# Two transformer blocks on one core: x loaded in halves on two queues, high parts multiplied first, and split turns at each norm

## The chip, the cores and the metric

The kernel runs on one core of one Trainium2 chip, in one launch. The metric is the device time of that launch in microseconds (us), as the median of several runs. TensorE (PE) multiplies, VectorE (DVE) and ScalarE (ACT) do elementwise work, GpSimd (POOL) does some elementwise work and issues transfers, SyncE (SP) issues transfers. All numbers are float32.

## The reference

256 rows of 1024 features pass through two blocks. The first block has two layers, the second one has one; every stage adds to the residual h.

```python
hn = rmsnorm(h, mix_norm[0])                 # y = x * rsqrt(mean(x*x) + eps) * g
h = h + moba_nsa_mixer(hn, ...)              # 8 causal heads + 8 heads of three gated branches
h = h + sqrelu_mlp(rmsnorm(h, ...), w1, w2)  # relu(h @ w1)**2 @ w2, 4096 hidden
h = h + fox_mixer(rmsnorm(h, ...), ...)      # 16 heads with a forget bias
h = h + sqrelu_mlp(rmsnorm(h, ...), w1, w2)
h = rmsnorm(h, final_norm)
# second block: shifts, scales and gates come from silu(c) @ w_ada + b_ada
h = h + 0.5 * gt1 * swiglu(modulate(rmsnorm(h, g1), sh1, sc1), ...)       # 2816 hidden
h = h + gt2 * hybrid_mixer(modulate(rmsnorm(h, gm), sh2, sc2), ...)       # pooling + dilated attention
h = h + 0.5 * gt3 * swiglu(modulate(rmsnorm(h, g2), sh3, sc3), ...)
out = rmsnorm(h, g_final)
```

In the three-branch (NSA) heads, each branch's softmax is multiplied by its own gate, sigmoid of a projection; one branch attends to 15 compressed blocks. With 256 rows, the block selections select everything that is causal.

## The kernel before, in words

The rows are two tiles of 128 (t = 0, 1). Weights arrive as 174 units of 128 x 2048 float32 (1 MB) in a ring of four buffers; unit u is loaded as soon as unit u - 4 has been used (`unit_used`). A float32 product is made of three passes in fp32r: every operand is split into a high part (rounded) and a low part (the rest), and high x low, low x high and high x high are summed (`three`, L1531 to L1534; L1563 and L1564 in the wide form). ScalarE rounds the weights (`round_half`, half a unit, L683; `advance`, a whole unit, L694), VectorE subtracts to get the rest (`rest_half`, L1050; L1061). `hi_ready` and `lo_ready` count the halves done.

Each norm needs, for each row tile: sums of squares on ScalarE (L705), a root and some polishing on VectorE (`inverse_root`), the scaling of the rows (`scale`: L1100 on VectorE in the first norm, L761 on ScalarE in the others, in pieces of 256, 256 and 512 columns), the turn of the rows by eight transposes in four chunks of 256 features (`turn_rows`, L1630), and out of the turned banks a high part on ScalarE (L746, or L748 and L753 where a shift is added) and a low part on VectorE (L1167, or L1154 and L1163). `act_high` counts high parts, `act_split` counts low parts, a chunk at a time. In the first norm ("mix0") the chunks of both row tiles are interleaved.

The products right behind a norm are `first_rows` (before the MLP and SwiGLU stages, through `begin_hidden`) and the value units (`value_part`, through `begin_values`, before the mixers; the first mixer, `v_even`, has its own order in the program of TensorE, L1772 to L1788). All of them wait for a chunk's low part before its first product, and the turn of row tile 1 stands in one piece among the products of row tile 0.

The opening: SyncE issues x's tile 0, the two halves of the first weight unit and x's tile 1 (L520 to L524), then further units. ScalarE issues the small tables, GpSimd the tables of the relative bias. Until the data land, TensorE does 22 warm-up products (L1774).

A mixer runs in ticks (a half or a quarter of a unit each). A plan, `plan`, writes out for each tick which heads' scores are made (`s`), which are turned (`t`), which are multiplied with the values (`pv`) and which output tiles are closed (`closed`); a closed tile is split by ScalarE (L838) and VectorE (L1253) one tick later. In a tick VectorE first does the logits of the tick's heads (L1226), then copies, weight halves, reciprocals, `extras`, and closed tiles. For the 16 gated heads VectorE multiplies the sum of the exponentials by 1 + exp(-z) and takes the reciprocal (L1246, L1247); GpSimd multiplies the probabilities by it (L565). The compressed branch has extras: its scores are taken over and shifted at tick ("km0", 2) (L1426 to L1433), exponentiated and weighed at ("km0", 3) (L959, L1434 to L1445), and turned by TensorE at the ticks of `CT_AT` (L1859).

## Time and profile before

| | us |
|---|---|
| median of three runs | 1103.0 (1101.99 to 1103.15) |
| the profiled execution's own time | 1100.71 |
| its span, first to last instruction | 1098.9 |
| TensorE busy | 1075.3 |
| VectorE busy | 779.2 |
| ScalarE busy | 662.0 |

The profile is of one execution. Times in the rows count from the first instruction. A row of the timeline has its start, its length, the engine, the line, the operation, what it writes and reads, its shape, and in square brackets the idle time of that engine just before it with what ended it. Rows of the same line that follow one another are merged (x8), and a matmul's length is modelled and overlaps the next.

### The profile page before, as it was taken

The page shows a single profiled execution, that of the slowest core. Times are in us where ns is not written, and L with a number is a line of the kernel's source. Part 1 is how long each engine was busy: PE and PEld are TensorE (multiplying, and loading weights), DVE is VectorE, ACT ScalarE, POOL GpSimd, SP SyncE. Part 2 cuts the span into 40 slices and gives each one's busy share as a digit, 9 for nine tenths or more (in the row PEclk, how much of TensorE's full clock was granted, in tenths as well). Part 3 has the DMA queues.
Part 4 walks back from the last instruction along what each step waited for, and adds up shares of the span by engine and source line. Part 5 has one row for each costly group of instructions (what it writes and reads, how often), then busy time and mean ns, then how long its engine had stood idle before and what let it go on. Part 6 is the DMA issues. An engine that isn't in the chain of part 4 may idle for free.

```text
span 1098.9 us, 15922 instructions
## 1 busy us (share of the span) xinstructions
PE 1075.3 (98%) x6102; PEld 915.4 (83%) x6102; DVE 779.2 (71%) x1272; ACT 662.0 (60%) x1071; POOL 112.8 (10%) x209
## 2 busy tenths in 40 slices
PE   8999999999999999999999999999999999999997
PEld 7988788888888997888888788888878977888885
DVE  6667667877777776676766778887875766565566
ACT  6667677565576776766565764354475766444443
POOL 1032201010100531020000000101000100000000
PEclk9999999999999999999999999999999999999999
DMA  8842348878764632687778457768545445555551
GB/s 337 298 160 78 116 154 319 301 283 316 289 217 174 227 123 108 210 322 267 273 254 340 153 204 284 295 253 318 198 153 178 149 144 182 191 191 181 185 185 65
DMA packets 40620, 238.31 MB, mean 217 GB/s; under 512 B 4661, under 2 KB 5845, under 8 KB 17632
## 3 DMA queue, kind: packets, MB, share of 16 engines
q1 hardware_dynamic: 26784, 188.81, 48.1%
q0 software_dynamic: 13040, 47.85, 11.6%
q8 instruction: 49, 0.80, 0.3%
q10 hardware_dynamic: 720, 0.62, 0.2%
q14 instruction: 27, 0.22, 0.1%
HBM read 236.15 MB, written 1.11 MB: 216 GB/s over the span
## 4 chain that ended last, share of the span: by engine, by line
PE 80%; DVE 9%; ACT 6%; issue 3%; DMA 1%; DVEq 0%; SPq 0%; ACTq 0%
PE bank L1563 21%; PE bank L1532 15%; PE bank L1534 14%; PE bank L1533 14%; PE bank L1564 10%; DVE w_lo L1061 2%; PE bank L1726 1%; PE bank L1708 1%; DMA raw<-in_stream 1%; DVE ada_raw L1296 1%; DVE w_lo L1050 1%; ACT w_hi L683 1%; ACT w_hi L694 1%; PE bank L1700 1%; ACT tok L705 1%
## 5 line engine op out<-in xcount | busy, mean ns | idle before, releaser
L1563 PE MATMUL bank<-a_two,w_hi 128*128 128x512 f32 x1088 | 386.9, 399 | 0.8 <-DVE w_lo L1061 0.8
L1061 DVE TENSOR_TENSOR w_lo<-raw,w_hi 128x2048 fp32r<-128x2048 f32 x122 | 278.5, 2303 | 105.3 <-ACT w_hi L694 105.3
L1564 PE MATMUL bank<-a_two,w_lo 128*128 128x256 f32 x1088 | 305.3, 281 | 0.0
L694 ACT ACTIVATE w_hi<-raw 128x2048 fp32r<-128x2048 f32 x122 | 232.2, 1910 | 63.0 <-DMA raw<-in_stream 62.9
L1563 PEld LDWEIGHTS bank<-a_two,w_hi 128*128 128x128 f32 x1088 | 204.4, 188 | 51.1 <-issue 1.3
L1564 PEld LDWEIGHTS bank<-a_two,w_lo 128*128 128x128 f32 x1088 | 205.5, 189 | 1.7
L1532 PE MATMUL bank<-w_lo,hid_hi 128*128 128x512 f32 x432 | 169.5, 392 | 0.1
L1533 PE MATMUL bank<-w_hi,hid_lo 128*128 128x512 f32 x432 | 168.6, 390 | 0.0
L1534 PE MATMUL bank<-w_hi,hid_hi 128*128 128x512 f32 x432 | 168.4, 390 | 0.0
L866 ACT ACTIVATE cross<-bank 128x256 f32<-128x256 f32 x136 | 51.5, 381 | 187.0 <-PE bank L1564 186.6
L1050 DVE TENSOR_TENSOR w_lo<-raw,w_hi 128x1024 fp32r<-128x1024 f32 x104 | 125.4, 1224 | 25.5 <-ACT w_hi L683 25.0
L683 ACT ACTIVATE w_hi<-raw 128x1024 fp32r<-128x1024 f32 x104 | 106.5, 1050 | 21.2 <-DMA raw<-in_stream 20.9
L1532 PEld LDWEIGHTS bank<-w_lo,hid_hi 128*128 128x128 f32 x432 | 81.1, 188 | 18.9 <-DVE hid_lo L1268 1.0
L1534 PEld LDWEIGHTS bank<-w_hi,hid_hi 128*128 128x128 f32 x432 | 81.1, 188 | 17.8
L1533 PEld LDWEIGHTS bank<-w_hi,hid_lo 128*128 128x128 f32 x432 | 81.1, 188 | 15.2
L1532 PE MATMUL bank<-a_two,w_hi 128*128 128x256 f32 x320 | 93.5, 292 | 0.0
L1534 PE MATMUL bank<-a_two,w_hi 128*128 128x256 f32 x320 | 90.4, 283 | 0.0
L1533 PE MATMUL bank<-a_two,w_lo 128*128 128x256 f32 x320 | 90.4, 282 | 0.0
L1296 DVE CUSTOM_DVE_ANT_0 ada_raw<-ada_raw,silu_row 128x1024 f32<-128x1024 f32 x72 | 84.8, 1219 | 5.2 <-DMA ada_raw<-in_ada 3.5
L1261 DVE TENSOR_TENSOR hid_act<-bank,cross 128x256 f32<-128x256 f32 x96 | 39.1, 420 | 56.5 <-ACT cross L866 56.5
L580 POOL DMA_DIRECT2D ada_raw<-in_ada x72 | 38.1, 530 | 325.9 <-DVE modc L1296 325.9
L1532 PE MATMUL bank<-w_lo,a_two 128*128 128x512 f32 (+1 forms) x160 | 62.1, 388 | 6.1 <-DVE a_two L1167 3.0
(215 smaller groups left out, 1490.3 us busy)
## 6 DMA issues: line engine op xcount, KB each, us to landing
raw<-in_stream SPq DMA_DIRECT2D x173, 1024.0 KB, 4.9
ada_raw<-in_ada POOLq DMA_DIRECT2D x72, 512.0 KB, 5.1
cmpw<-in_stream SPq DMA_DIRECT2D x4, 1024.0 KB, 7.0
rel_band<-rel_scratch POOLq DMA_DIRECT2D x2, 1024.0 KB, 10.6
cum_row<-cum_scratch POOLq DMA_DIRECT2D x4, 512.0 KB, 5.3
gate_row<-gate_scratch POOLq DMA_DIRECT2D x3, 512.0 KB, 5.6
h<-in_x SPq DMA_DIRECT2D x2, 512.0 KB, 5.9
raw<-in_stream SPq DMA_DIRECT2D x2, 512.0 KB, 6.6
```

Of the source, the lines that this page charges most:

```text
L683: nc.scalar.activation(w_hi[:, u % RING, part_], raw[:, u % RING, part_], ACT.Copy).then_inc(hi_ready, 1)
L694: nc.scalar.activation(w_hi[:, u % RING, :], raw[:, u % RING, :], ACT.Copy).then_inc(hi_ready, 2)
L866: nc.scalar.activation(cross[:, slot, nt, :], ps[bank][:, T:2 * T], ACT.Copy).then_inc(done, 1)
L1050: nc.vector.tensor_tensor(w_lo[:, u % RING, part_], raw[:, u % RING, part_], w_hi[:, u % RING, part_].bitcast(F32), ALU.subtract).then_inc ...
L1061: nc.vector.tensor_tensor(w_lo[:, u % RING, :], raw[:, u % RING, :], w_hi[:, u % RING, :].bitcast(F32), ALU.subtract).then_inc(lo_ready, 2)
L1261: nc.vector.tensor_tensor(to[:, nt * T:(nt + 1) * T], ps[bank][:, 0:T], cross[:, slot, nt, :], ALU.add).then_inc(done, 1)
L1296: nc.vector.tensor_tensor_reduce(part, part, silu_row[:, :], 1.0, 0.0, ALU.mult, ALU.add, modc[:, p:p + 1]).then_inc(ada_done, 1)
L1532: nc.tensor.matmul(dst, l_hi, r_lo, start=start, stop=False)
L1533: nc.tensor.matmul(dst, l_lo, r_hi, start=False, stop=False)
L1534: return nc.tensor.matmul(dst, l_hi, r_hi, start=False, stop=stop)
L1563: nc.tensor.matmul(ps[bank][:, 0:2 * T], wh[:, k, cols_], a_two[:, :, k, :], start=k == 0, stop=False)
L1564: ins = nc.tensor.matmul(ps[bank][:, T:2 * T], wl[:, k, cols_], a_hi[:, k, :], start=False, stop=k == KT - 1)
```

## The change

- x is loaded in four pieces (row tile by column half): the first halves on SyncE's queue, the second ones on ScalarE's, where the bias pick table and the second half of the first weight unit go too. VectorE takes the squares of tile 0's second half. Both tiles are scaled before the first chunk is turned.
- In the opening, `first_value` is now `opening`: it does the terms of one k and one row tile in a given order; "h" is high x high, "r" is high x low weights, "l" is low x high weights. Only "l" waits for the chunk's low part. `first_rows` does the two high terms before it waits for the low part.
- Tile 1's turn is in two calls, chunks 0 and 1 and chunks 2 and 3, with part of the last chunk of tile 0 ahead of and between them.
- With a shift, VectorE does a shift and a low part in turn.
- `close_tiles` moves the second of two tiles closed in one tick to the next tick, except in the last two ticks.
- The gate is kept as 1 / (1 + exp(-z)) and is a second factor in GpSimd's operation.
- The compressed branch's steps are one or two ticks later.
- 19 warm-up products in place of 22.

```diff
-WARM = 22
+WARM = 19
@@ close_tiles
+    for tick, later, last in reversed(list(zip(ticks, ticks[1:], ticks[2:]))):
+        if len(tick.closed) == 2:
+            later.closed = [tick.closed.pop()] + later.closed
...
-CT_AT = [("km1", 0, 1), ("km1", 0, 2), ("qm1", 0, 0), ("qm1", 0, 1)]
+CT_AT = [("km1", 0, 2), ("km1", 0, 3), ("qm1", 0, 0), ("qm1", 0, 1)]
@@ SyncE
-            sp.dma_start(h[:, 0, :], x[0:P, :]).then_inc(x_landed[0], 16)
-            for part in range(2):
-                part_ = slice(HALF * part, HALF * part + HALF)
-                sp.dma_start(raw[:, 0, part_], stream[0][:, part_]).then_inc(first_landed[part], 16)
-            sp.dma_start(h[:, 1, :], x[P:T, :]).then_inc(x_landed[1], 16)
+            sp.dma_start(h[:, 0, 0:512], x[0:P, 0:512]).then_inc(x_landed[0][0], 16)
+            sp.dma_start(h[:, 1, 0:512], x[P:T, 0:512]).then_inc(x_landed[1][0], 16)
+            sp.dma_start(raw[:, 0, 0:HALF], stream[0][:, 0:HALF]).then_inc(first_landed[0], 16)
@@ GpSimd
-                        ins = pool.tensor_scalar(p_, p_, wgt[:, 2 * i + t:2 * i + t + 1], 1.0, ALU.mult, ALU.mult)
+                        gate = 1.0 if heads[i][5] is None else gates[:, t, heads[i][5]:heads[i][5] + 1]
+                        ins = pool.tensor_scalar(p_, p_, wgt[:, 2 * i + t:2 * i + t + 1], gate, ALU.mult, ALU.mult)
@@ ScalarE, opening
+            act.dma_start(h[:, 0, 512:D], x[0:P, 512:D]).then_inc(x_landed[0][1], 16)
             act.dma_start(par[:, 0:COLS["pool_scale"]], cols[:, 0:COLS["pool_scale"]]).then_inc(norms_landed, 16)
             act.wait_ge(dve_step, 1)
+            nc.scalar.activation(stat[:, 10, :], stat[:, 9, :], ACT.Sqrt)
+            act.dma_start(h[:, 1, 512:D], x[P:T, 512:D]).then_inc(x_landed[1][1], 16)
+            act.dma_start(rpick[:, :], rel_pick).then_inc(pick_landed, 16)
+            act.dma_start(raw[:, 0, HALF:UNIT], stream[0][:, HALF:UNIT]).then_inc(first_landed[1], 16)
-            squares("mix0", 0)
+            act.wait_ge(x_landed[0][0], 16)
+            nc.scalar.activation(tok[:, 0, 0:512], h[:, 0, 0:512], ACT.Square, scale=1.0 / 32, accum_out=stat[:, 0, 0:1]).then_inc(sumsq, 2)
+            root("mix0", 0)
+            square_half("mix0", 1, 0)
+            square_half("mix0", 1, 1)
+            root("mix0", 1)
...
-                if tick.at("km0", 0, 3):
+                if tick.at("km1", 0, 0):
                     act.wait_ge(cshifted, 1)
@@ VectorE, turned
-                if shift is not None and chunks[0] == 0:
-                    for c in (1, 3):
+                for c in chunks:
+                    if shift is not None and c < 2:
+                        odd = 2 * c + 1
...
@@ VectorE, mixer: 16 gated heads
-                            chain(nc.vector.tensor_tensor(w, inv_gates[:, :, gate], d, ALU.mult))
-                            nc.vector.reciprocal(w, w).then_inc(weight_ready, 1)
+                        nc.vector.reciprocal(wgt[:, 2 * i:2 * i + 2], den[:, 2 * i:2 * i + 2]).then_inc(weight_ready, 1)
@@ VectorE, opening
+            dve.wait_ge(x_landed[0][1], 16)
+            chain(nc.vector.tensor_tensor_reduce(tok[:, 0, 512:D], h[:, 0, 512:D], h[:, 0, 512:D], 1.0 / D, 0.0, ALU.mult, ALU.add,
+                                                 stat[:, 1, 0:1]))
             inverse_root("mix0", 0)
             scale("mix0", 0)
+            inverse_root("mix0", 1)
+            scale("mix0", 1)
             rest_half()
...
-                if tick.at("km0", 0, 2):
+                if tick.at("km0", 0, 3):
                     dve.wait_ge(cscores, 1)
-                if tick.at("km0", 0, 3):
+                if tick.at("km1", 0, 1):
                     dve.wait_ge(cprobs, 1)
@@ TensorE, first_rows
+                pe.wait_ge(act_high, TURN[name] + 4 * t + 2 * j + half + 1)
+                for k in [2 * half + n for n in ks]:
+                    nc.tensor.matmul(dst, a_hi[:, 4 * j + k, ts], wh[:, k, :], start=j == 0 and k == 0, stop=False)
+                    nc.tensor.matmul(dst, a_hi[:, 4 * j + k, ts], wl[:, k, :], start=False, stop=False)
                 pe.wait_ge(act_split, TURN[name] + 4 * t + 2 * j + half + 1)
...
@@ TensorE, begin_hidden
-                turn_rows(name, 1)
-                first_rows(name, u, 1, 0, 1)
+                first_rows(name, u, 1, 0, 1, (0,))
+                turn_rows(name, 1, (0, 1))
+                first_rows(name, u, 1, 0, 1, (1,))
+                turn_rows(name, 1, (2, 3))
@@ TensorE, begin_values: in the same way with opening(..., ns=(0,)) and opening(..., ns=(1,))
...
@@ TensorE, opening of v_even
-            first_value(j=0, part=0)
-            first_value(j=0, part=1)
-            pe.wait_ge(pick_landed, 32)
+            pe.wait_ge(pick_landed, 16)
+            pe.wait_ge(relt_landed, 16)
             pe.wait_ge(pool_step, 1)
             nc.tensor.matmul(ps[6][0:16, 0:REL], relt[:, :], rpick[:, :], start=True, stop=True).then_inc(rel_rows, 1)
+            first_value = partial(opening, "mix0", "v_even", width=V1W)
+            first_value(0, 0, 0, "h")
             turn_rows("mix0", 1)
+            first_value(0, 0, 0, "rl")
+            first_value(0, 0, 1, "hlr")
             pe.wait_ge(rel_rows_sb, 1)
+            first_value(0, 1, 0, "hr")
+            first_value(0, 1, 1, "hr")
+            first_value(0, 1, 0, "l")
+            first_value(0, 1, 1, "l").then_inc(unit_used, 1)
+            for k in range(2):
+                for t in range(TT):
+                    ins = first_value(1, t, k)
+            ins.then_inc(unit_used, 1)
```

## Rows read from the trace of the kernel before

**Rows 1.** The page, busy time of each engine, its share, instructions.

```profile
PE 1075.3 (98%) x6102; PEld 915.4 (83%) x6102; DVE 779.2 (71%) x1272; ACT 662.0 (60%) x1071; POOL 112.8 (10%) x209
```

**Rows 2.** Windows: length; busy PE, PEld, DVE, ACT, POOL; granted clock, DMA share, GB/s.

```profile
4.50:6.00 1.50, 1.50 (x15) 1.50 (x15) 0.15 (x1) 1.29 (x4) 1.36 (x1) 1.00 1.00 235
...
14.00:16.60 2.60, 0.77 (x8) 0.56 (x6) 0.77 (x3) 2.60 (x7) 0.49 (x1) 1.00 0.97 404
```

**Rows 3.** Timeline of all engines, 0 to 30 us.

```profile
4.71 0.63 ACT L705 ACTIVATE tok<-h 128x512 f32<-128x512 f32 x1 [2.04 <-DMA h<-in_x]
...
7.18 0.88 DVE L1100 TENSOR_SCALAR tok<-h,stat 128x512 f32<-128x512 f32 x2
7.19 1.06 ACT L683 ACTIVATE w_hi<-raw 128x1024 fp32r<-128x1024 f32 x1 [0.75 <-DMA raw<-in_stream]
...
8.28 1.23 DVE L1050 TENSOR_TENSOR w_lo<-raw,w_hi 128x1024 fp32r<-128x1024 f32 x1 [0.21 <-ACT w_hi L683]
8.54 0.62 ACT L746 ACTIVATE a_two<-bank,par 128x128 fp32r<-128x128 f32 x2 [0.30 <-PE bank L1630]
...
9.42 0.60 DVE L1167 SCALAR_TENSOR_TENSOR a_two<-bank,par,a_two 128x128 fp32r<-128x128 f32 x2
...
10.08 0.50 PE L1532 MATMUL bank<-w_lo,a_two 128*128 128x512 f32 x1 [1.20 <-DVE a_two L1167]
...
13.66 1.09 PE L1630 MATMUL bank<-par,tok 128*128 128x128 f32 x8
...
16.59 0.47 PE L1532 MATMUL bank<-w_lo,a_two 128*128 128x512 f32 x1 [1.83 <-DVE a_two L1167]
...
24.00 2.28 DVE L1061 TENSOR_TENSOR w_lo<-raw,w_hi 128x2048 fp32r<-128x2048 f32 x1
```

**Rows 4.** The tile h in 0 to 15 us: its two transfers.

```profile
DMA to landing us min/median/max: 3.9/5.9/7.8
```

**Rows 5.** Windows as in rows 2, and ScalarE's timeline, unit 6.

```profile
24.00:26.00 2.00, 2.00 (x13) 1.75 (x12) 2.00 (x2) 1.15 (x2) 0.00 (x0) 1.00 0.73 229
...
35.03 1.06 ACT L683 ACTIVATE w_hi<-raw 128x1024 fp32r<-128x1024 f32 x1 [4.69 <-DMA raw<-in_stream]
```

**Rows 6.** TensorE's timeline at the turn of tile 1, norm mlp0.

```profile
150.05 0.83 PE L1630 MATMUL bank<-par,tok 128*128 128x128 f32 x4
...
151.05 0.66 PE L1630 MATMUL bank<-par,tok 128*128 128x128 f32 x4 [0.17 <-ACT tok L761]
151.47 0.47 PE L1532 MATMUL bank<-w_lo,a_two 128*128 128x512 f32 x1
```

**Rows 7.** Timelines of TensorE and ScalarE in the norm gmix.

```profile
816.51 0.50 PE L1532 MATMUL bank<-w_lo,a_two 128*128 128x512 f32 x1 [0.75 <-DVE a_two L1163]
...
821.32 0.84 PE L1630 MATMUL bank<-par,tok 128*128 128x128 f32 x4 [0.42 <-ACT tok L761]
...
823.00 0.72 ACT L753 ACTIVATE a_two<-shifted 128x256 fp32r<-128x256 f32 x2
...
824.22 0.42 PE L1532 MATMUL bank<-w_lo,a_two 128*128 128x512 f32 x1
```

**Rows 8.** Timelines of TensorE and VectorE, even mixer, ticks km0 and km1.

```profile
84.38 0.84 DVE L1429 TENSOR_TENSOR pc<-bank,pc 128x240 f32<-128x240 f32 x2
...
86.80 0.36 PE L1699 MATMUL bank<-k_two,q_two 128*128 128x256 f32 x1 [1.42 <-DVE low L1226]
...
88.00 0.40 DVE L1437 TENSOR_REDUCE den<-pc 128x16 f32<-128x240 f32 x1
...
92.24 0.60 PE L1859 MATMUL bank<-par,pc 128*15 128x128 f32 x4
```

**Rows 9.** Timelines of VectorE and TensorE, fox mixer.

```profile
414.32 0.76 DVE L1253 TENSOR_TENSOR q_two<-bank,q_two 128x256 fp32r<-128x256 f32 x2
...
415.78 0.36 PE L1699 MATMUL bank<-k_two,q_two 128*128 128x256 f32 x1 [1.07 <-DVE low L1226]
```

**Rows 10.** GpSimd's timeline, even mixer.

```profile
88.16 0.83 POOL L565 TENSOR_SCALAR prob<-prob,wgt 128x256 f32<-128x256 f32 x2 [3.69 <-DVE wgt L1247]
```

More of the change, by code:

```diff
@@ L1593, in turn_hidden, with row_part @@
                 ins.then_inc(hid_turned, 1)
-            def row_part(u, banks, l_hi, l_lo, width, start, stop, part, parts, by_rows=False, sums=False, opening=False):
+            def row_part(u, banks, l_hi, l_lo, width, start, stop, part, parts, by_rows=False, sums=False):
                 wh = w_hi[:, u % RING, 0:2 * width].rearrange("p (k c) -> p k c", k=2)
@@ L1599, in row_part @@
                 four = [(t, n) for t in range(TT) for n in range(2)]
-                if opening:
-                    order = [(k, t, n) for t in range(TT) for k in range(2) for n in range(2)]
-                elif by_rows:
+                if by_rows:
                     order = [(k, t, n) for t, n in four for k in range(2)]
@@ L1937, in _ @@
             mlp("mlp0", "mix1")
-            begin_values("mix1", lambda j, part: value_part("mix1", "v_fox", j, part, 4))
+            begin_values("mix1", "v_fox")
             def fox_extras(tick):
@@ L1960, in _ @@
             glu("glu0", "gmix")
[L1961 removed]
+            begin_values("gmix", "uv_dil")
             def dil_extras(tick):
```

106 lines of the change are left out of this document (56 added, 50 removed).

## The prediction

> **What bounds the kernel now.** I read the page's busy shares first: TensorE is busy for 1075.3 of the 1098.9 us span and VectorE for 779.2 [rows 1]. A matmul's modelled end overlaps its successor, so the share alone hides waits. I therefore read the list of who waited for whom and then TensorE's timeline at the places it names. Steady 512-column products start 0.228 us apart, 256-column ones 0.118 us, and against that pitch the trace has few gaps: the opening, the half turn that repeats in each norm, and some waits inside the two attention mixers. Everywhere else a change on another engine is worth nothing. The change touches exactly these places.
>
> The opening is a latency chain. The first x tile lands at about 4.7, its squares, root and scaling run until 8.06, eight transposes, a rounding and a split follow, and the first product starts at 10.08 [rows 3]. x's second tile, issued behind both weight halves, lands 7.8 us after its issue at 2.11 [rows 4]. Its turn starts at 13.66 and its product at 16.59; TensorE does 0.77 us of work in 14.0 to 16.6 [rows 2, 3]. From 16.59 it streams without a gap to the end of v_even at 31.8, 15.2 us for three and a half units, so 4.34 a unit (0.36 for one term of one k and one row tile).
>
> **Opening, part by part.** x goes in four pieces of 256 KB on two queues, ahead of the weights. The first two together are the 512 KB that now land at 4.7, so I keep 4.7 for them. The other two come 0.35 and 0.6 MB later. The windows show 235 GB/s in 4.5 to 6.0 and 404 in 14.0 to 16.6 [rows 2], so I put tile 1 whole at 6.7 to 7.4, against 9.9 now. The price: 0.5 MB of x, the small tables and half of the other queue now stand ahead of the first weight half, which today lands at 7.15 [rows 3]; at 400 GB/s that is 8.0 to 9.4.
>
> VectorE takes one half of tile 0's squares. Nearest is its own 128x512 multiply with sum, 0.69 in the fused norm, beside ScalarE's 0.63 plus 0.19: both are done by 5.5, where two ScalarE halves end at 6.05 now. Root, reciprocal and two polishing steps take 1.0; tile 0 is scaled from 6.8, tile 1's root follows, and tile 1 is scaled by 9.9 to 10.2 (two halves take 0.88). Then ScalarE rounds the first half (1.06) [rows 3] from 8.2 to 9.4, turns chunk 0 (0.62), rounds the second half, copies the bias rows (0.59) and turns tile 1's chunk. The first product needs only the rounded half and the high part, so it starts at 10.0 to 11.1, no earlier than now. Tile 1's turn comes right behind it at 10.3 to 11.5, against 13.66.
>
> VectorE becomes the late one. In order it owes: the rest of half 1 (1.22), chunk 0's split (0.60), the rest of half 2, two more chunk splits, then the rests of unit 1 with a split between [rows 3]. That gives unit 0 done at 15.5 (early landing) or 16.1 (late), against 16.59 plus 2.15 = 18.7. Units 1 and 2 follow at 4.34 each; unit 3 waits for its 2.28 us rest, which starts at 24.0 now [rows 3] and would start at 21.9 or 22.9. End of v_even: 28.6 or 29.6, against 31.8. The opening saves 3.2 or 2.2; I take 2.6.
>
> What is late next: the weights of unit 6, for which ScalarE waits 4.69 us until 35.03 [rows 5]. Their issue waits for unit 2, so it moves with TensorE, and the queues are not full in 24 to 26 (229 GB/s) [rows 5]; by the same bytes they land at about 32. ScalarE's and VectorE's full stretch from there to the first scores at 52.7 shifts with it. I take off 0.1 for what is not passed on: 2.5. Bounds 0.5 (everything lands 2 us later than I say) and 4.
>
> The three warm-up products fewer end at about 6.9; nothing waits for them. The rest of the weight halves moved one slot is a reordering of equal work.
>
> **The half turn, six times.** In every norm after the first, TensorE turns tile 1 in one go: four transposes in 0.40, then it stands until ScalarE has scaled columns 512 to 1023, then four more. At 150.05 the second four start at 151.05: 0.60 idle, and 151.47 is the next product [rows 6]. Now one k of the last chunk (0.69) goes ahead of the turn and one k between its halves. In mlp0, mix1 and mlp1 TensorE reached the turn with everything ready, so the whole 0.60 is covered: from 150.05, product to 150.74, four transposes to 151.14, product to 151.83, transposes to 152.25; today that point is 151.47 + 1.38 = 152.85. Tile 1's high part would be ready by 151.65 and its split by 152.2, where the first products need it at 152.25 and, with high parts first, only at 153.2. 3 x 0.60 = 1.8.
>
> In gf1, gmix and gf2 there is a shift too. The first product of tile 0 waits for the low part: in gmix it starts at 816.51 [rows 7], 1.14 behind the product before it, of which 0.91 is not pitch. With high parts first that wait goes, but it buys nothing by itself: the turn of tile 1 waits for ScalarE's scaling at 821.32 [rows 7], and that chain starts from sums and squares which TensorE no longer drives. The idle time moves from ahead of tile 0 to ahead of the turn. What is gained is behind it: tile 1's first product waits now for work order (824.22) and then for ScalarE's rounding of chunk 0, 823.00 + 0.37 plus a hop, 823.5 [rows 7]: 0.72. The same reading gives 0.80 in gf1 (632.79 against 631.98) and 0.74 in gf2 (911.64 against 910.90). VectorE's shifts now stand between the splits, which delays its later adds by 0.08, counted. Sum 2.3; with the others 4.1. Bounds: 3.0 if the later steps hand back 0.2 each, 5.0 if the first waits count too.
>
> **Mixers.** Fox: two closed tiles cost VectorE 0.76 ahead of the logits for which TensorE waits 1.07 [rows 9]. Closing one there and one a tick later takes off 0.38; the deferred one falls in front of logits that are not awaited. 0.4. In the dilated mixer no wait follows its double close: 0.
>
> Even: the compressed scores' four operations (84.38 to 86.10) stand ahead of the logits that cost TensorE 1.42 at 86.80 [rows 8]. A tick later they wait for nothing, and that 1.42 goes, as does 0.60 at 91.88 behind it. But the weighing of the compressed heads, 1.93 from 88.00 [rows 8], moves two ticks while its reader moves one. By my count VectorE reaches it at 93.1 and ends at 95.05; TensorE gets to the transposes at 93.4 and stands 1.7. Net 2.0 - 1.7 - 0.2 of logits = 0.1. Bounds -0.8 and +1.6.
>
> The gate goes from VectorE (one chained operation of about 0.2 for each of 16 heads) to a second per-row scalar on GpSimd. Its two operations take 0.83 [rows 10] and their reader comes 5 us later, so neither saving nor a doubling reaches the path: 0, between -0.5 and +0.3.
>
> **Sum.** 2.5 + 4.1 + 0.4 + 0.1 = 7.1. On the profiled execution (span 1098.9, its time 1100.7) that is a span of 1091.8. The median of the three runs is 1103.0, 2.3 above the profiled time; I take the difference as it is: 1095.9.
>
> **A rule about two queues.** The Trainium skill, DMA: Bandwidth & Descriptors, Issuing engines are not separate DMA queues, says that transfers started by different engines share the same 16 DMA engines and interleave, so that a second starter only saves issue time. By that rule the second queue lands nothing sooner in total, and x's halves are paid for by the weights: the late end of my opening, 2.2. The trace has only tiny transfers on the second queue and neither confirms nor contradicts it.
>
> **Rivals.**
> The opening gives nothing. First product no earlier, weights later, VectorE full. For it: the order of VectorE's list, and 2 KB rows where there were 4 KB. Against: tile 1 is now missing for 3.7 us and that is removed in every version. Saving 0.3 + 4.6 = 4.9: 1098.1.
>
> The even mixer takes it back. The stall at the transposes grows when unit weights arrive late: up to 0.8 net loss, and with the opening at 2.0: 5.7 saved, 1097.3.
>
> The clock falls in the opening, the case on the slower side. TensorE would stand with short work between 6.9 and 13. If it were granted half speed there and kept it while v_even streams, the 15.2 us of work from 16.59 to 31.8 would take 30.4: 1103.0 - 7.1 + 15.2 = 1111. The balance is nought where 7.1 us of full-speed work, about half of that stretch, run at 1.2 GHz. Against it: 1.00 is granted from the start and through 14.0 to 16.6 [rows 2], with a stand of 1.8. The new stands are each no longer. The Trainium skill, TensorE: Matmul & The Clock Gate, What's actually happening, says that half speed is the idle state and that activity lifts it; the granted clock in these rows never shows that state.
>
> The change doesn't do what it says: the transfers on ScalarE's queue go out only behind its table load (1.28) and land as late as now. Then tile 1 lands at 9.9 and blocks ScalarE's first rounding; the opening saves 1: 1097.4.
>
> **Chances.** Forecast 0.60, opening gives nothing 0.12, even mixer 0.10, late second queue 0.10, clock 0.03; 0.05 for what I don't see. A measurement tells 0.2% (2.2 us) from nothing. The likeliest case alone runs from 1094 to 1098; with the unknown bounds (savings of 3.4 to 9.8) the range is 1093.2 to 1099.6. Faster 0.89, same 0.07, slower 0.04.
>
> **What would show it.** Tile 1's transposes at 10.3 to 11.5 and v_even's end before 30; no idle between the halves of tile 1's turn in six norms; in the three shifted norms an idle stretch of about 1 us ahead of that turn; the 1.42 at the even mixer gone and one of 1 to 2 us ahead of the compressed transposes. It is wrong if v_even ends past 31, if the granted clock drops, or if the first score of the even mixer keeps its place though v_even ends early.

## The result and the profile after

The changed kernel takes 1107.2 us (median of 14 runs, 1103.67 to 1109.66), the kernel before 1102.67 in the same session: ratio 1.0035, 95% interval 1.0025 to 1.0046. It is slower by 0.35%; 1095.9 was forecast. All fourteen executions have a mean granted clock of 0.991 to 0.997; the two at 0.997 took 1103.7 and 1104.2, the others 1105.0 to 1109.7. The profiled execution took 1107.36 us.

The page of the changed kernel; the busy line answers to [rows 1]. TensorE is busy 2.5 us more, for the same products, and the span is 6.5 longer.

```profile
span 1105.4 us, 15921 instructions
...
PE 1077.8 (98%) x6096; PEld 918.8 (83%) x6096; DVE 778.3 (70%) x1259; ACT 664.3 (60%) x1069; POOL 113.9 (10%) x208
```

The list of who waited for whom on TensorE (total, times, longest). The first, second, fourth and fifth rows were not there before: TensorE waits for the weights' rest `w_lo` in `first_rows` (L1592) and `opening` (L1700), for the relative-position pick, and for the compressed heads' probabilities `pc`.

```profile
PE bank L1592 <- DVE w_lo L1062: 5.0, 4, 2.1
PE bank L1818 <- DMA rpick<-in_rel_pick: 3.0, 1, 3.0
PE bank L1748 <- ACT probT L822: 2.1, 2, 1.9
PE bank L1700 <- DVE w_lo L1062: 1.8, 2, 1.5
PE bank L1903 <- DVE pc L1455: 1.4, 1, 1.4
```

**The opening.** The tile h: four transfers now, from 3.7 to 9.1 us from issue to landing, where [rows 4] had 3.9 to 7.8.

```profile
DMA to landing us min/median/max: 3.7/4.1/9.1
```

TensorE's timeline, answering to [rows 3] (turn of tile 0, pick, first product, turn of tile 1, end of v_even).

```profile
7.39 1.06 PE L1644 MATMUL bank<-par,tok 128*128 128x128 f32 x8 [0.44 <-DVE tok L1112]
11.44 1.88 PE L1818 MATMUL bank<-rpick,relt 33*16 33x511 f32 x2 [2.99 <-DMA rpick<-in_rel_pick]
13.53 1.00 PE L1700 MATMUL bank<-w_hi,a_two 128*128 128x512 f32 x2 [0.21 <-ACT a_two L748]
14.33 1.91 PE L1644 MATMUL bank<-par,tok 128*128 128x128 f32 x8
...
33.71 0.28 PE L1543 MATMUL bank<-a_two,w_hi 128*128 128x256 f32 x1
```

ScalarE's timeline. It stands 4.19 us for x's last quarter, then 1.78 for the second weight half.

```profile
10.81 0.63 ACT L707 ACTIVATE tok<-h 128x512 f32<-128x512 f32 x1 [4.19 <-DMA h<-in_x]
...
15.17 1.06 ACT L685 ACTIVATE w_hi<-raw 128x1024 fp32r<-128x1024 f32 x1 [1.78 <-DMA raw<-in_stream]
```

Windows, columns as in [rows 2]. The granted clock (the third number from the end) goes to 0.50, which is 1.2 GHz, late in a stand of TensorE from 8.5 to 11.4. In [rows 2] it was 1.00 at 14.0 to 16.6. v_even ends at 33.71 instead of 31.81.

```profile
9.00:10.00 1.00, 0.00 (x0) 0.00 (x0) 0.00 (x0) 0.00 (x0) 0.00 (x0) 1.00 1.02 422
10.00:12.00 2.00, 0.56 (x1) 0.12 (x2) 0.21 (x1) 1.09 (x4) 0.00 (x0) 0.71 1.02 419
12.00:14.00 2.00, 1.79 (x3) 0.50 (x2) 1.86 (x6) 1.39 (x3) 0.00 (x0) 0.50 1.04 428
14.00:16.60 2.60, 2.60 (x12) 2.40 (x12) 1.56 (x4) 1.43 (x2) 0.00 (x0) 0.50 0.99 410
```

**The norms.** TensorE at tile 1's turn in mlp0, answering to [rows 6]. The idle between the halves is gone, but 152.76, the product now ahead of the turn, starts 0.59 behind its pitch (0.82 behind the product before it, where 0.23 is usual), waiting for `w_lo`.

```profile
151.71 0.61 PE L1596 MATMUL bank<-w_hi,a_two 128*128 128x512 f32 x2
152.76 0.50 PE L1592 MATMUL bank<-w_hi,a_two 128*128 128x512 f32 x1 [0.43 <-DVE w_lo L1062]
...
153.57 0.60 PE L1644 MATMUL bank<-par,tok 128*128 128x128 f32 x4
```

VectorE makes that `w_lo` only behind tile 1's inverse root, whose last operation starts at 151.41:

```profile
151.48 1.22 DVE L1062 TENSOR_TENSOR w_lo<-raw,w_hi 128x1024 fp32r<-128x1024 f32 x1
```

TensorE in gmix, answering to [rows 7]. The product waits until 825.41, and the turn starts at 825.98. ScalarE starts scaling the tile at 824.25. Before, the turn was at 821.32; this stage starts 3.49 later here, so that is 824.81 in this trace, and the turn is 1.17 late. Counted in the same way it is 1.43 late in gf1 and 1.40 in gf2.

```profile
822.73 1.14 PE L1700 MATMUL bank<-w_hi,a_two 128*128 128x512 f32 x3
825.41 0.50 PE L1700 MATMUL bank<-w_lo,a_two 128*128 128x512 f32 x1 [1.53 <-DVE w_lo L1062]
...
825.98 0.60 PE L1644 MATMUL bank<-par,tok 128*128 128x128 f32 x4
...
827.51 1.06 PE L1644 MATMUL bank<-par,tok 128*128 128x128 f32 x4
```

The clock falls behind that stand too, and in gf2 from 915 to 919, but not in gf1, where the stand is 2.1:

```profile
823.00:825.00 2.00, 0.85 (x3) 0.19 (x1) 1.32 (x4) 1.25 (x4) 0.00 (x0) 1.00 0.19 78
...
827.00:829.00 2.00, 2.00 (x8) 1.61 (x7) 1.16 (x5) 1.75 (x5) 0.13 (x1) 0.50 0.00 0
```

**Mixers.** A wait of 1.40 at the compressed transposes ([rows 8]) came as forecast, and the fox wait ([rows 9]) fell from 1.07 to 0.74. The stretch that holds it (to mlp1, below) is only 0.15 to 0.2 shorter by the fox edit: 115.74 to 115.55 in e4, 115.32 to 115.17 from e3 to e8.

```profile
97.31 0.61 PE L1903 MATMUL bank<-par,pc 128*15 128x128 f32 x4 [1.40 <-DVE pc L1455]
...
417.55 0.36 PE L1739 MATMUL bank<-k_two,q_two 128*128 128x256 f32 x1 [0.74 <-DVE low L1238]
```

**Where the time went.** TensorE's timeline cut at v_even's end, at tile 0's turn in each norm, and at the last product. Lengths in us; three of the columns are experiments told below, and e13 has the mixers' edits too.

| stretch | before | change | norms only (e2) | rest last (e3) | both mended (e13) |
|---|---|---|---|---|---|
| start to v_even's end | 31.81 | 33.71 | 32.30 | 33.45 | 29.25 |
| to mlp0 | 111.88 | 112.10 | 112.65 | 113.99 | 112.09 |
| to mix1 | 180.55 | 180.67 | 180.67 | 180.22 | 180.18 |
| to mlp1 | 115.74 | 115.43 | 115.57 | 115.32 | 115.17 |
| to gf1 | 182.19 | 182.63 | 182.49 | 182.30 | 182.15 |
| to gmix | 190.54 | 191.66 | 191.52 | 190.62 | 190.53 |
| to gf2 | 87.40 | 88.79 | 88.95 | 87.30 | 87.29 |
| to the last product | 191.13 | 192.68 | 193.33 | 190.96 | 191.10 |

The opening costs 1.90, the last three rows, behind the norms with a shift, 4.06.

### The profile page after: what moved, and what is told of

Its sections match the earlier page's. It is cut to its first block, busy times and chain, and to the rows that moved or that the text cites. A ratio compares the mean times of both kernels' runs of the same rounds, so it can differ in the third digit from the quotient of the medians.

```text
span 1105.4 us, 15921 instructions
## 1 busy us (share of the span) xinstructions
PE 1077.8 (98%) x6096; PEld 918.8 (83%) x6096; DVE 778.3 (70%) x1259; ACT 664.3 (60%) x1069; POOL 113.9 (10%) x208
## 3 DMA queue, kind: packets, MB, share of 16 engines
q10 hardware_dynamic: 1196, 1.74, 0.4%
## 4 chain that ended last, share of the span: by engine, by line
PE 79%; DVE 10%; ACT 5%; issue 3%; DMA 2%; ACTq 0%; SPq 0%; DVEq 0%
PE bank L1574 19%; PE bank L1543 13%; PE bank L1545 13%; PE bank L1544 13%; PE bank L1575 10%; PE bank L1700 2%; DVE w_lo L1073 2%; DMA raw<-in_stream 2%; ACT w_hi L696 2%; DVE w_lo L1062 2%; PE bank L1766 1%; PE bank L1748 1%; DVE ada_raw L1303 1%; ACT tok L707 1%; DMA h<-in_x 1%
## 5 line engine op out<-in xcount | busy, mean ns | idle before, releaser
L1574 PEld LDWEIGHTS bank<-a_two,w_hi 128*128 128x128 f32 x1088 | 204.4, 188 | 51.2 <-issue 1.5
L1544 PEld LDWEIGHTS bank<-w_hi,hid_lo 128*128 128x128 f32 x432 | 81.1, 188 | 15.2
L1543 PEld LDWEIGHTS bank<-a_two,w_hi 128*128 128x128 f32 x320 | 61.1, 191 | 2.1 <-issue 1.9
```

What stands on the lines that cost most here:

```text
L1543: nc.tensor.matmul(dst, l_hi, r_lo, start=start, stop=False)
L1544: nc.tensor.matmul(dst, l_lo, r_hi, start=False, stop=False)
L1574: nc.tensor.matmul(ps[bank][:, 0:2 * T], wh[:, k, cols_], a_two[:, :, k, :], start=k == 0, stop=False)
```

## The experiments

All parts below are hunks of the change's own diff put on the kernel before, unless a diff or a sentence says otherwise. The ratios are to the kernel before on the same chip.

**e1: the new opening alone.** Edit: the transfers, the order of both halves and of the terms in mix0, `WARM = 19`.

> The kernel before with the new opening alone (x in four pieces on two queues, high parts first, VectorE's half of the squares, 19 warm-up products); norms, mixers and gate as before. Theory A, from the changed kernel's trace: what is put on ScalarE's queue is starved (x's last quarter lands at 10.8, the relative-position pick at 11.4, the second weight half at 15.2), TensorE stands, its clock falls to half from about 11 to 17, and v_even ends at 33.7 instead of 31.8; of these 1.9 us some 1.3 to 2.1 reach the end: 1104.0 to 1104.8, ratio 1.0012 to 1.0019. Rival B: the opening's loss is hidden by ScalarE's wait of 4.7 us for weights, and the whole loss is the norms': 1102.7 within 0.5. The prediction on record would have 1100.2.

Measured: 1.0001 (0.9991 to 1.0012). x's last quarter is used at 10.26, v_even ends at 34.25, the clock is 0.50 from 12 to 19. The mechanism is there, but its loss against the median of the kernel before is not: theory A's time is at the edge of the interval, rival B's holds. e4 shows why.

**e2: the new norm order alone.** Edit: `begin_hidden`, `begin_values`, `first_rows`, VectorE's shifts between the splits.

> The kernel before with the new norm order alone (one k of the last chunk ahead of tile 1's turn, one between its halves, high parts first, shifts between splits); opening, mixers and gate as before. Theory A: the product that was moved ahead of the turn needs the rest of the weights (w_lo) of its half, which VectorE makes only after the inverse root of tile 1; so TensorE waits 0.6 in mlp0, mix1 and mlp1, where it was to save 0.6, and in gf1, gmix and gf2 the turn comes 1.2 to 1.4 late against the work before it. Together 0 from the first three and 1.0 to 1.4 lost in each of the last three, of which part is given back behind: 2 to 4.4 us lost, 1104.7 to 1107.1, ratio 1.002 to 1.004. Rival B, the prediction on record: 4.1 us saved, 1098.6, ratio 0.9963, and the loss of the change is the opening's alone. Rival C: the norms' gain and loss cancel, 1102.7 within 0.5.

Measured: 1.0027 (1.0016 to 1.0037), 3.0 us slower. Theory A; the forecast saving of 4.1 is excluded. TensorE waits for `w_lo` in all six norms: 0.4, 0.2 and 0.4 idle in the first three, 2.1, 1.5 and 2.05 in the shifted ones.

**e3: the rest term last.** The diff is condensed; `begin_values` is changed in the same way.

```
-                first_rows(name, u, 1, 0, 1, (0,))
-                turn_rows(name, 1, (0, 1))
-                first_rows(name, u, 1, 0, 1, (1,))
-                turn_rows(name, 1, (2, 3))
+                if name in SHIFTS:
+                    piece("hl"); turn_rows(name, 1, (0, 1)); piece("r"); turn_rows(name, 1, (2, 3))
+                else:
+                    turn_rows(name, 1, (0, 1)); piece("hl"); turn_rows(name, 1, (2, 3)); piece("r")
```

> As the norm order alone, but the last chunk's products go by term: where there is a shift the high and low rows times the high weights ahead of tile 1's turn and the rows times the weights' rest (w_lo) between its halves; in mlp0, mix1 and mlp1 tile 1's first half is turned first, then the terms with high weights, its second half, then the rest term. Nothing that needs w_lo stands ahead of the turn. Theory A (w_lo is what failed): the 0.60 of each of the first three and the 0.72 to 0.80 of the others come out as forecast, 3.5 to 4.1 us saved: 1098.6 to 1099.2, ratio 0.9963 to 0.9968. Rival B: TensorE stands for another reason (ScalarE's scaling and rounding set tile 1's products in any order), and the result is 1101.5 to 1103.5. Rival C: high parts first or the shifts between the splits cost something by themselves: slower than before by 0.5 us or more.

Measured: 0.9980 (0.9968 to 0.9992), 2.0 us faster. Only the order of the same products and of their waits differs from e2, so the cause of the norms' loss is shown: it is a product that needs `w_lo` ahead of the turn. The saving is half of the forecast. In the table above the stretches behind the norms give less still: e3's are 0.33, 0.42, -0.11, -0.08, 0.10 and 0.17 shorter than before, 0.8 in all, nearly all of it from the first three norms. In mlp0 the turn goes like this, and the second half's turn follows work:

```profile
153.79 0.83 PE L1639 MATMUL bank<-par,tok 128*128 128x128 f32 x4
154.38 1.17 PE L1588 MATMUL bank<-w_hi,a_two 128*128 128x512 f32 x4
155.39 0.60 PE L1639 MATMUL bank<-par,tok 128*128 128x128 f32 x4
```

In the shifted norms the first product of tile 1 comes 2.24 behind its turn, where it came 2.90 behind in gmix before (824.22 against 821.32), but most of it is handed back soon: 0.7 ten us later in gf1 and gf2, and in gmix all but 0.1 by the next norm. In gf1 it is at the turn of the hidden rows:

```profile
644.54 0.44 PE L1601 MATMUL bank<-par,hid_act 128*128 128x128 f32 x2 [0.54 <-DVE hid_act L1304]
```

**e4: the mixers' edits alone.** Edit: `CT_AT` and the compressed heads' ticks, `close_tiles`, `gates` on GpSimd.

> The kernel before with the mixers' three edits alone: tiles closed singly, the compressed heads' steps one or two ticks later, the gate on GpSimd. The prediction on record: fox 0.4 saved, even 0.1 lost or gained, gate 0: 1102.3, ratio 0.9996. From the changed kernel's trace: the even mixer's two waits of 1.4 and 0.6 are gone and a wait of 1.8 at the compressed transposes has come, fox saves 0.33; if the 2.1 us wait for turned probabilities near 64 there comes from weights that land late behind the late opening, it is absent here and the result is 1102.2 within 0.4. Rival: that wait comes from the moved compressed steps or the gate on GpSimd, is here too, and the result is 1103.5 to 1104.5.

Measured: 0.9987 (0.9974 to 1.0). The wait near 64 (1.9 in the change) is absent, as it is in other profiles with either opening: 1.5 to 2.4 in e2, e3, e7, e11, e12 and e15, absent in e1, e5, e6, e8, e10 and e13. From v_even's end to mlp0 this profile has 111.25 and e8's 111.24, against 111.88 before; but e5, which has the old mixer and v_even's end at 32.15 as e8 has it, takes 111.37. So the even mixer saves 0.1 to 0.6. The profile holds the surprise. The opening here is that of the kernel before, yet:

```profile
16.00:18.00 2.00, 0.64 (x2) 0.58 (x3) 1.40 (x3) 2.00 (x7) 0.19 (x1) 0.67 1.04 419
18.00:20.00 2.00, 2.00 (x8) 1.71 (x7) 2.00 (x5) 2.00 (x8) 0.00 (x0) 0.50 0.99 408
...
35.38 0.28 PE L1532 MATMUL bank<-a_two,w_hi 128*128 128x256 f32 x1
```

The clock falls with the stand of 1.83, here from 15.6 to 17.4. In six profiles with the old opening v_even ends at 31.81, 32.15, 32.30, 33.39, 33.45 and 35.38, and the last three have the fall. The profile on which the prediction rests was a lucky one (1100.7, where medians of 1102.3 to 1103.4 were measured).

What such a fall is worth can be read from the mean granted clock of every execution, which is on record for 118 executions of the kernel before on four chips. In 61 of them it is 0.998 or more, with a median time of 1102.0; in 57 it is lower, with a median of 1104.1. The falls, with whatever goes with them, cost 2.1 us in about half of the executions. Against the undisturbed ones on its chip (1101.9) e1, in which no execution reaches 0.998, is 1.6 slower, as its theory A had it.

The three parts alone (e1, e2, e4) multiply to 1.0015, and the whole change is at 1.0035. The 2.2 us between them are within the intervals, and no run explains them.

**e5: the kernel before, its two stands filled.**

```
             turn_rows("mix0", 0)
+            fill(3, 0)
...
             turn_rows("mix0", 1)
+            fill(5, 3)
```

> The kernel before with eight more warm-up products in its opening, three behind tile 0's turn and five behind tile 1's, in the two stands of TensorE (1.2 and 1.8 us in the trace of before). Theory A: the opening of before loses its clock behind the second stand in many executions (two of three profiles of it show 0.5 from about 17 to 20 or 22, v_even ends at 33.5 and 35.4 there, at 31.8 and 32.3 where the clock stays at 1.00), and short work in the stands keeps it: v_even ends near 32 and the median falls by 1 to 2 us, 1101.4 to 1102.4, ratio 0.998 to 0.999. Rival B: the clock falls there whatever TensorE does, 1103.4 within 0.7.

Measured: 0.9987 (0.9975 to 1.0). Clock 1.00 up to the tail, v_even ends at 32.15, runs from 1100.09 to 1102.58 instead of 1100.1 to 1109.3. All twelve executions have a mean clock of 0.998 or more, and their median, 1101.8, is that of the kernel before's undisturbed executions on this chip. Theory A: the ratio is at the interval's edge, and what the fill removes is the executions with a fall.

**e6: the new opening, its transfers elsewhere.**

```
 act: h[:, 0, 512:D]
+act: h[:, 1, 512:D]        (ahead of par and the table load; it stood behind them)
-act: rpick                 +pool: rpick
-act: raw second half       +sp: raw second half, behind the first
```

> The new opening alone, with its transfers put elsewhere: both halves of x for ScalarE's queue ahead of par and the table load, the pick on GpSimd's queue as before the change, the second weight half on SyncE's queue behind the first. Theory A: what stood in the new opening was three transfers starved on ScalarE's queue behind 4 MB of SyncE's; issued early or on the full queue they land in time: x whole by 6.7 to 7.5, second half rounded by 10.5, tile 1's turn at 9.5 to 11, v_even ends at 28.5 to 31, and 1.5 to 2.5 us are saved against the kernel before: 1100.9 to 1101.9. Rival B: the clock falls in the opening all the same and takes the gain back, v_even ends past 31.5: 1102.5 to 1103.5. Rival C: the transfers on ScalarE's queue are as late as they were, x's last quarter past 9.

Measured: 0.9981 (0.9971 to 0.9992), 1100.3 us. ScalarE's and TensorE's timelines, a window of 10 to 12, and what waits at the first scores:

```profile
6.30 0.61 ACT L705 ACTIVATE tok<-h 128x512 f32<-128x512 f32 x1
...
8.52 1.06 ACT L683 ACTIVATE w_hi<-raw 128x1024 fp32r<-128x1024 f32 x1 [0.71 <-DMA raw<-in_stream]
8.82 1.09 PE L1641 MATMUL bank<-par,tok 128*128 128x128 f32 x8 [0.85 <-DMA par<-in_cols]
...
10.80 0.63 PE L1695 MATMUL bank<-w_hi,a_two 128*128 128x512 f32 x2
...
29.07 0.28 PE L1543 MATMUL bank<-a_two,w_hi 128*128 128x256 f32 x1
...
33.77 1.06 ACT L683 ACTIVATE w_hi<-raw 128x1024 fp32r<-128x1024 f32 x1 [4.30 <-DMA raw<-in_stream]
...
51.46 0.36 PE L1732 MATMUL bank<-k_two,q_two 128*128 128x256 f32 x1 [1.47 <-DVE q_two L1215]
```

```profile
10.00:12.00 2.00, 2.00 (x11) 1.16 (x10) 2.00 (x4) 1.70 (x4) 0.00 (x0) 1.00 1.03 434
```

x's last quarter, issued at 1.18, is used at 6.30; in the change it was issued at 1.72, just behind SyncE's first weights (1.65), and landed at 10.8. v_even ends at 29.07, between the forecast's 28.6 and 29.6. But unit 6's weights came only 1.26 sooner (33.77 against 35.03 in [rows 5]), and TensorE stands 1.47 ahead of the first scores: of the 2.74 gained, 1.25 is left at mlp0.

Three transfers moved at once here; e11 and e13 below differ in the order of par and x's last quarter alone. Why it was late can be read from the two queues' packets in the change, here from 8 to 10.8 us (packets, MB, share of the engines' time; q1 is SyncE's, q10 ScalarE's):

```profile
q1 hardware_dynamic: 113, 0.80, 69.3%
q10 hardware_dynamic: 119, 0.33, 29.9%
```

The queues had equal numbers of packets served, but ScalarE's were smaller (2.8 KB on average against 7.1), so it got 29% of the bytes. From 5.5 to 8 it was 129 packets with 0.59 MB against 120 with 0.23 MB. No run changes the size of the packets, so this is read from the trace and not tested.

**e7: the changed norm order, TensorE kept busy.** Eight products are repeated ahead of the one that waits, so the sums are not those of the reference. In gmix it is `opening(..., "h")` four times.

```
+                    for _n in range(8):
+                        nc.tensor.matmul(ps[BEGIN_BANKS[0]][:, :], a_hi[:, 4, 0:P], wh[:, 2, :], start=False, stop=False)
```

> The norm order as changed (as in the run of the norms alone), with eight 128x512 products repeated ahead of the product that waits for w_lo in gf1, gmix and gf2; this changes the sums, and is only for the time. Theory A: the stand of 1.5 to 2.1 us at w_lo lets the clock fall to half behind it (825 to 829 and 913 to 918 in the norms alone), which costs more than the wait itself; with TensorE busy through the stand the clock stays at 1.00 in both and 2 to 3.5 us of the 3.0 that the norms lost come back: 1103 to 1104.3. Rival B: the clock has nothing to do with it, the loss is the wait alone: 1106.3 within 0.7.

Measured: 1.0027 (1.0016 to 1.0038), as e2. The clock did hold: first this kernel in gmix, then e2.

```profile
825.00:827.00 2.00, 2.00 (x12) 1.66 (x11) 0.68 (x2) 1.33 (x4) 0.00 (x0) 1.00 0.00 0
```

```profile
825.00:827.00 2.00, 2.00 (x8) 1.65 (x7) 0.86 (x3) 1.39 (x4) 0.00 (x0) 0.51 0.00 0
```

Its stretches from gmix to the end are 2.1 shorter than e2's, but the ratio is not smaller. The stretches after each norm still sum to 3.1 us over the kernel before. Half of e7's executions, five, have a mean clock of 0.998 or more; their median is 1104.4, 2.6 over the kernel before's undisturbed ones on this chip (1101.8). So with the clock held the wait alone costs 2.6 of the norms' 3.0. The other five have 1106.0: in the profile the clock falls in the opening, which e7 leaves as it was. Theory A's return of 2 to 3.5 us is not borne out; a share of up to 1.6 us for the clock in the norms is within the intervals.

**e8: norms with the rest last, and the mixers.** Edit: e3's and e4's together.

> The opening of before, the norm order with the rest term last, and the mixers' three edits. Alone they saved 2.0 and 1.5 us. If they add: 1099.9 (1099.2 to 1100.6), ratio 0.9968. If the mixers' gain is a matter of chance in the opening and not of their edits, no better than the norms alone: 1101.3.

Measured: 0.9982 (0.9969 to 0.9995), no better than e3. The traces give the even mixer 0.1 to 0.6 and fox 0.15 to 0.2, less than these intervals resolve; the 1.4 that e4's ratio gives was too large a reading.

**e9: the new opening on one queue.** Edit: the four quarters of x and both weight halves on SyncE's.

> The new opening alone, all four quarters of x and both weight halves on SyncE's queue in that order, only par on ScalarE's, the pick on GpSimd's. Theory A: what the opening gains comes from the order of the transfers, not from a second queue: x whole by 6.5 to 7.5, v_even ends at 28.5 to 30, 1100.0 to 1101.0, ratio 0.998 to 0.999, as in the run with the two queues put right. Rival B: the second queue was what brought x early (1.2 us of issues saved): x whole past 7.5, v_even ends past 30.5, 1101.5 or more.

Measured: 0.9999 (0.9986 to 1.0012). x is whole at 7.13, as theory A had it, so its order brings x early on one queue too. But the first weights, issued at 2.57 instead of 1.64, are rounded at 9.65, 1.13 later than in e6; TensorE stands 1.75 ahead of its first product, the clock falls late in that stand, and v_even ends at 31.08. The end of v_even and the time are rival B's: the second queue brings the 0.9 us of issues that it saves. The intervals of e6 and e9 overlap a little. This profile also stands 2.2 at the first scores, at 55; ScalarE had waited for weights until 37.42.


```profile
12.00:14.00 2.00, 2.00 (x11) 2.00 (x10) 1.70 (x4) 1.37 (x5) 0.49 (x1) 0.50 1.02 430
```

**e10: the whole change, transfers as in e6.**

> The whole change with only its transfers put right, as in the opening run with the queues put right. The opening alone went from 1.0001 to 0.9981 by this (2.2 us at medians); if that adds to the whole change (1.0035), 1.0014 to 1.0020, 1104 to 1104.7; what is left is the norms' 3 us less the mixers' gain. Rival: the norms' wait absorbs an earlier opening and nothing comes of it, 1.003 or more.

Measured: 1.0002 (0.9991 to 1.0013), better than expected (1.0014 to 1.0020). The starved transfers are worth 0.0033 of the change, 3.6 us, by two runs on different chips.

**e11: all mended, par second on ScalarE's queue.**

```
 act: h[:, 0, 512:D]
+act: par                  (ahead of x's last quarter)
 act: h[:, 1, 512:D]
```

> The change with the transfers put right (par second on ScalarE's queue), the norm order with the rest term last, and the mixers' edits. By the segments of the traces: opening 2.1 to 3, norms 0.8 to 2.0, fox 0.33, even 0.2: 3.5 to 5 us below the kernel before, ratio 0.9955 to 0.9968. Rival: the parts overlap (weights that land late ahead of the even mixer take back the opening's gain), 2.5 us, 0.9977.

Measured: 0.9983 (0.9972 to 0.9995): a miss, and the most telling one. par was moved up because tile 0's turn waited 0.85 for it in e6; this put x's last quarter third, and it starved again:

```profile
9.81 0.63 ACT L709 ACTIVATE tok<-h 128x512 f32<-128x512 f32 x1 [3.39 <-DMA h<-in_x]
```

The clock is 0.50 from 11 to 18 and v_even ends at 33.37.

**e12: the same with the compressed heads' steps where they were.**

> As the run with everything mended, with the compressed heads' steps where they were. By the traces the moved steps remove waits of 1.6 and 0.8 (less 0.4) and add one of 1.8, so 0.2 us in their favour: this one 0 to 0.5 us slower than that. Rival: with the opening early the added wait is larger and this one is the faster by 0.5 or more.

Measured: 0.9988 (0.9978 to 0.9998), not told apart from e11. In its trace the waits of 1.3 at the scores and 0.6 behind them are back and the one of 1.4 at the compressed transposes is gone.

**e13: the opening of e6, the norms of e3, the mixers' edits.**

> The change with the transfers exactly as in the opening run with the queues put right (x's last quarter second on ScalarE's queue, par third) and the norm order with the rest term last. If the causes are the two named and they add: the whole change with the queues put right gave 1.0002, the norms' order is worth 0.0047 between its two forms (1.0027 and 0.9980): 0.9955 (0.9945 to 0.9968), 1098 to 1099.5; x's last quarter lands before 7, v_even ends near 29.3, no fall of the clock before the tail. Rival: they don't add, 0.9975 or more, because weights that land late ahead of the even mixer (a stand of 2.3 us near 63 in some profiles) take it back.

Measured: 0.9951 (0.9939 to 0.9963), 1097.5 us against 1102.5: 5.0 us faster than the kernel before and 9.7 below the change's own median (of another session). The causes add: e6, e3 and e4 multiply to 0.9948. Two differences are clean. From e10 to e13 only the order of terms in the norms changes: 1.0002 to 0.9951. From e11 to e13 only the issues of par and x's last quarter are exchanged, 0.5 us apart: 0.9983 to 0.9951, 3.5 us. All five executions have a mean clock of 0.998 or more, where a third of the kernel before's on this chip (6 of 17) do not; against its undisturbed ones (1102.1) e13 is 4.6 faster. Clock 1.00 up to the tail; TensorE in gmix:

```profile
817.98 0.83 PE L1650 MATMUL bank<-par,tok 128*128 128x128 f32 x4 [0.25 <-ACT tok L765]
818.57 0.73 PE L1716 MATMUL bank<-w_lo,a_two 128*128 128x512 f32 x2
819.14 0.60 PE L1650 MATMUL bank<-par,tok 128*128 128x128 f32 x4
820.22 0.70 PE L1716 MATMUL bank<-w_hi,a_two 128*128 128x512 f32 x2 [0.48 <-ACT a_two L757]
```

**e14: e13 with par on SyncE's queue and four more warm-up products.**

> As the run with both mended, with par on SyncE's queue ahead of the first weight half and four warm-up products in the stands ahead of the first product. If par's landing at 8.8 to 9.2 is what holds tile 0's turn: turn at 7.2 to 7.6, but the first weight half lands 0.3 later and the first product waits for it: v_even ends within 0.4 of that run's, and the median within 0.5. If the stand between lets the clock fall in part of the executions, as before, the median is lower than that run's by 0.5 to 1 only thanks to the fill, and the spread narrower.

Measured: 0.9963 (0.9951 to 0.9975), 1098.7. Turn of tile 0 at 7.89, v_even's end at 29.0, and no gain: 1.2 slower at the medians, where within 0.5 was forecast. e13 loses no clock in its stands that the fill could give back. In e14's profile TensorE stands 1.74 at the first scores, against 0.90 in e13's.

**e15: the new opening as changed, kept busy.** Edit: `fill(9, 0)` behind tile 0's turn, `fill(3, 0)` ahead of the first product, `fill(2, 3)` behind tile 1's turn.

> The new opening alone, as changed (starved transfers), with 14 more warm-up products: nine in the stand behind tile 0's turn, three ahead of the first product, two behind tile 1's turn. Theory A: the fall of the clock (0.5 from 11 to 17) doubles some 4 us of work and costs 1.5 to 2.5 of the opening's loss; kept busy, the clock stays at 1.00, v_even ends at 31.5 to 32.5 instead of 34 and the median is 1.0 to 2.0 us below that of the kernel before. Rival B: the late transfers set the time of every step up to v_even's end anyway, and it stays at 33.5 to 34.5 though the clock stays up: ratio 1.000.

Measured: 1.0003 (0.9994 to 1.0013). The trace goes with theory A (clock 1.00, v_even's end at 31.84) and the time with rival B. All twelve executions have a mean clock of 0.998 or more, and their median, 1103.2, is still 1.1 over the kernel before's undisturbed ones on this chip (1102.1). In this profile TensorE waits 1.4 us for late weights here, and 1.5 near 64, where ScalarE had waited 1.1 for weights:

```profile
616.48 0.47 PE L1543 MATMUL bank<-w_lo,hid_hi 128*128 128x512 f32 x1 [1.40 <-DVE w_lo L1069]
```

Whether the earlier v_even causes these waits or chance does isn't settled.

## Why the prediction was wrong

**Opening, saving 2.5: failed at the landing of tile 1.** "I put tile 1 whole at 6.7 to 7.4" rested on total bytes at 400 GB/s, as if everything landed in the order of its issue, over both queues. From 9 to 16.6 us the rows show 410 to 428 GB/s moved, as assumed, but most of it for SyncE's queue: the three transfers issued on ScalarE's at 1.72, 2.14 and 2.80 landed at about 10.8, 11.4 and 15.2. The pick's landing, for which TensorE stood 2.99, had no term in the working at all. The order of issue across queues, 0.5 us one way or the other, decided 3 to 5 us of landing: x's last quarter is there at 5.8 to 6.2 in e6, e10, e13 and e14, and at 8.8 to 10.8 in the change, e1, e11, e12 and e15. The rest of the step was right: with the transfers early v_even ends at 29.07. The rule of the Trainium skill, DMA: Bandwidth & Descriptors, Issuing engines are not separate DMA queues, that a second starter saves issue time only, agrees with these traces: e9 against e6 shows 0.9 us of issues saved and the first weights 1.1 sooner. That pieces land in the order of issue over both queues was read into it; the trace of the change shows 29% of the bytes for ScalarE's queue from 8 to 10.8.

**"I take off 0.1 for what is not passed on": mis-sized.** TensorE's stand at the first scores is 1.47 in e6 and 0.90 in e13. The prediction moved unit 6's landing by the whole gain, to 32; it came at 33.77.

**The half turn, saving 4.1: failed at what the moved product waits for.** The working covered the 0.60 by a product and never asked for that product's operands. It needs `w_lo` of the last half, which VectorE makes behind tile 1's inverse root (151.48 in mlp0, 824.14 in gmix). In the first three norms the 0.6 saved is lost again (0.4 to 0.6); in the shifted three the turn, which sets the path, comes 1.2 to 1.4 late. Measured: 3.0 lost. "That chain starts from sums which TensorE no longer drives" was right, and this is why putting anything ahead of the turn that waits longer than the chain is a loss. With that term last, 2.0 saved of 4.1: the 0.66 in each shifted norm is there, but 0.6 to 0.7 of it is handed back in each, which the lower bound (3.0) had only at 0.2. By the stretches only the 0.8 from e3's trace is accounted for, most of it in the first three norms; where the rest of the 2.0 comes from stays open.

**Fox 0.4, even 0.1, gate 0: right in sign.** The fox wait fell by 0.33 but its stretch only by 0.15 to 0.2; the new stall at the transposes is 1.4 against 1.7 forecast; the even mixer saved 0.1 to 0.6, inside its bounds. No run has the gate alone.

**The rivals.** "Late second queue" (0.10) had the right queue and the wrong reason and size: the table load does not hold them (in the change x's last quarter is issued at 1.72 while the table load runs from 1.66 to 2.94, and in e11 at 1.65, ahead of it). The stream of weights beside them does, or their place on their own queue, which no run tells apart. x lands at 10.8, not 9.9. "The clock falls" (0.03) did happen, against a trace in which it seemed not to. Its price of 15.2 was too high: the clock was back within 7 us in every profile, and a fall is worth 2.1 us between executions of the kernel before, half of which have one. In e15 holding it was not enough, since the late transfers stayed. "1.00 is granted from the start" was a misreading as well. In the trace of before the granted clock prints as 1.00 in both of these windows, but it has no record ahead of 4.5 us, and the warm-up products start 0.213 us apart up to there and 0.112 behind it (14 in 3 us, then 20 in 2 us):

```profile
1.00:4.00 3.00, 2.95 (x14) 2.95 (x15) 0.02 (x2) 1.49 (x2) 2.67 (x4) 1.00 0.64 206
...
5.00:7.00 2.00, 2.00 (x20) 2.00 (x19) 0.76 (x5) 1.34 (x5) 0.86 (x1) 1.00 1.00 294
```

So this trace does show half speed at its start, which the prediction says it never shows.

No rival had the norms losing, which is what made the change slower. The range left out everything above 1099.6 because it took both large terms from one profile and one reading.

## What to carry to other kernels

When a product is moved ahead of a wait, list the semaphores of that product, not only of what it moves past; one that comes behind the wait's own chain turns the cover into the bound. Split it by terms and put only those ahead whose operands are old. A transfer on a second queue that is needed early should be issued before the first queue's stream starts. Take the base from several profiles: one with a clock fall missing makes a change look free of it. When executions of one kernel differ, sort them by their mean granted clock before comparing medians.

## What the runs showed of the hardware

With 1 MB transfers queued behind one another on SyncE's queue and 400 to 430 GB/s moved in all, 256 KB of x on ScalarE's queue landed 4.6 to 5.1 us after its issue at 1.17 or 1.18, ahead of the first weights (e6, e10, e13, e14), and 7.0 to 9.1 us after an issue at 1.65 to 1.72 (the change, e1, e11, e12, e15); 512 KB issued at 2.80 took 11 to 12.8. In the late cases x's last quarter was also the third transfer on its own queue, and no run tells the two apart. The 96 KB of par, third at 1.66, took 7.1 to 7.5; the pick, issued at 1.95 on GpSimd's queue behind 2 KB, took 6.6 in e6.

The granted clock of TensorE went from 1.00 to 0.50 during or just behind stands of 1.75 to 3.35 us in the opening. With the same old opening and a stand of 1.83 it did so in three of six profiles. It fell behind stands of 1.5 and 2.05 in gmix and gf2 and not behind one of 2.1 in gf1 (the change, e2, e10), and behind 2.07 and 2.3 near 65 (e11, e3) but not behind 2.4 (e2). So the length of the stand does not settle it. It held at 1.00 where short products filled the stand (e5, e7, e15), and was back at 1.00 some 3 to 7 us after it fell. Every profile shows 0.50 in its last 2 to 6 us, behind the last product. What stays open is why holding the clock in the norms, worth 2 us in the stretches of e7, does not show in the ratio of e7 against e2; intervals of 1.2 us either way can hide it.
